# Attention on one core: values held still in two column halves of the array, row sums by 32-column groups

## The reference, cut to what matters

```python
AT_HEADS, AT_KV_HEADS, AT_HD, Q_BLOCK = 8, 2, 64, 128
keys = concat([rope(ak), cache_k])          # 1024 + 128 keys, 2 key-value heads
def one(qblk):                              # 128 queries, 4 query heads per key-value head
    s = einsum('bqkgd,bskd->bkgqs', qblk, k) * D ** -0.5
    p = softmax(s, axis=-1)
    return einsum('bkgqs,bskd->bqkgd', p, v)
```

## Time and profile before

| what | value |
|---|---|
| median of three runs | 2380.0 us (2376.93 to 2381.06) |
| span of the profiled execution, first to last instruction | 2375.2 us |
| TensorE busy | 97% of the span |
| VectorE, ScalarE, GpSimd busy | 58%, 34%, 9% |
| the attention loop | 1156 to 1401 us |

### The profile page before, as it was taken

How to read it: one execution, slowest core, us unless ns; L and a number is a source line. 1 busy time by engine, 2 the same in 40 slices (tenths; PEclk the granted TensorE clock), 3 DMA queues, 4 the chain that set the end, 5 groups by cost and what they waited for, 6 DMA issues and landing times. The chain is left out here.

```text
span 2375.2 us, 44414 instructions
## 1 busy us (share of the span) xinstructions
PE 2301.3 (97%) x17959; PEld 2126.0 (90%) x17959; DVE 1388.8 (58%) x2203; ACT 810.0 (34%) x1398; POOL 224.3 (9%) x244
## 2 busy tenths in 40 slices
PE   6999999999999899999999999998999999999997
PEld 5887779999999889998999989877999999998886
DVE  4331266533554467665455546768676676667877
ACT  5321132213333233223344444325222223234444
POOL 0000000001110011112211101000121121120001
PEclk9999999999999999999999999999999999999999
DMA  6324632236452532214100228421222232259534
GB/s 279 120 84 182 224 111 107 101 135 202 157 173 85 196 107 90 80 67 158 44 18 13 88 107 311 159 91 62 78 105 91 73 109 91 73 177 273 131 100 124
DMA packets 126864, 295.40 MB, mean 124 GB/s; under 512 B 19808, under 2 KB 63280, under 8 KB 117376
## 3 DMA queue, kind: packets, MB, share of 16 engines
q1 hardware_dynamic: 93360, 236.31, 29.7%
q10 hardware_dynamic: 29392, 41.82, 4.8%
q0 software_dynamic: 3968, 15.21, 1.7%
HBM read 207.83 MB, written 85.53 MB: 124 GB/s over the span
## 5 line engine op out<-in xcount | busy, mean ns | idle before, releaser
L62 PE MATMUL ps<-prj_w,h_hi 128*128 128x512 f32 (+1 forms) x864 | 255.4, 380 | 4.1 <-DVE h_lo L755 4.1
L62 PE MATMUL ps<-h_hi,fill_whi 128*128 128x384 f32 x672 | 235.6, 351 | 4.7 <-ACT fill_st L1119 2.4
L62 PE MATMUL ps<-h_lo,fill_whi 128*128 128x384 f32 x672 | 226.5, 337 | 3.8 <-issue 3.8
L62 PE MATMUL ps<-wt 128*128 128x320 f32 (+2 forms) x1046 | 227.2, 327 | 2.3 <-DVE merged L3205 1.3
L62 PE MATMUL ps<-h_hi,fill_wlo 128*128 128x384 f32 x672 | 226.6, 337 | 0.1
L62 PE MATMUL ps<-ys,mergedr 128*128 128x256 f32 (+1 forms) x1056 | 219.6, 297 | 0.4 <-issue 0.4
L62 PE MATMUL ps<-zb,mergedr 128*128 128x320 f32 (+2 forms) x764 | 200.1, 326 | 4.9 <-issue 2.7
L62 PE MATMUL ps<-zb,wt 128*128 128x384 f32 (+3 forms) x758 | 200.2, 325 | 0.0
L62 PEld LDWEIGHTS ps<-prj_w,h_hi 128*128 128x128 f32 x864 | 158.3, 191 | 42.8 <-issue 10.6
L62 PEld LDWEIGHTS ps<-wt 128*128 128x128 f32 x1046 | 179.6, 189 | 16.7 <-issue 2.6
L62 PEld LDWEIGHTS ps<-ys,mergedr 128*128 128x128 f32 x1056 | 174.5, 190 | 0.7 <-issue 0.7
(11 more groups left out here) (502 smaller groups left out, 4675.5 us busy)
## 6 DMA issues: line engine op xcount, KB each, us to landing
wraw<-in_w_ffn_in SPq DMA_DIRECT2D x22, 1024.0 KB, 5.3
prj_raw<-in_w_ada SPq DMA_DIRECT2D x16, 1024.0 KB, 6.0
fill_raw<-in_w_fill SPq DMA_DIRECT2D x30, 512.0 KB, 4.4
wtf<-a_dram SPq DMA_DIRECT2D x55, 256.0 KB, 2.7
bg_dram<-fill_st ACTq DMA_DIRECT2D x72, 192.0 KB, 2.0
xf<-bg_dram POOLq DMA_DIRECT2D x24, 576.0 KB, 7.1
tok_dram<-prj_tst ACTq DMA_DIRECT2D x45, 256.0 KB, 2.1
prj_raw<-in_w_tok SPq DMA_DIRECT2D x10, 1024.0 KB, 6.9
```

Of the source, the lines that this page charges most:

```text
L62: mm = pe.matmul(out, lhs[a], rhs[b], start=first and n == 0, stop=last and n == 2, skip_group_check=onto)
```

## The change

The loop now runs over query tiles, not over groups: a step takes one key block for both key-value heads. In `values` the 64 value columns of a key-value head are stationary and 512 columns of exponentials move; head 0 writes partitions 0 to 63 and head 1 partitions 64 to 127 of the same bank, so the result comes out already turned. The row sums, which the column of ones gave before, come from `sums`: 32 columns of ones are stationary, and the 128 columns of exponentials of query head `a` move into partitions `32a` to `32a + 31`. After a tile VectorE inverts the sums of all heads (`inverted`), `spread_sums` copies each row to the 64 partitions of its head by eight small matmuls, ScalarE copies the unscaled result out (`output`), VectorE multiplies it by the spread sums (`normed`), and SP, not ScalarE, issues the transfer. Per tile, the queries' turn, the shifts' turn and all eight `shift_scores` for the next tile stand between the steps. So before the first tile all eight `shift_scores` are done, not four, each between two halves of a `branch` unit. Scores have two PSUM banks, not three. The hardware loops are written out.

```diff
+        def rows_out(s):                                   # SP
+            sp.dma_start(g.y_dram[...], yt[s % 2][:]).then_inc(sem[f"yout{s % 2}"], 16)
...
-            def scores(n, kv, j):
-                pe.wait_ge(sem["ex"], 9 * n + j + 1)
-                out, at = ps[:, ST + j % 3, :], slice(j * P, j * P + P)
+            def scores(i, kv, j):
+                u = 2 * NT * i + 2 * j + kv
+                if u >= 2:
+                    pe.wait_ge(sem["ex"], u - 1)
+                if j == 0:
+                    pe.wait_ge(sem["pte"], turn(i, 2 + kv) + 1)
+                out, at = ps[:, ST + kv, :], slice(j * P, j * P + P)
...
-            def values(n, kv, j):
-                pe.wait_ge(sem["ex"], 9 * n + j + 4)
-                for a in range(G):
-                    mm = pe.matmul(ps[:, OB, a * H1:a * H1 + H1], pt[j % 3][:, a * P:a * P + P], va[:, j, kv, :],
-                                   start=j == 0 and a == 0, stop=j == NT - 1 and a == G - 1)
+            def values(i, j):
+                n = NT * i + j
+                pe.wait_ge(sem["ex"], 2 * n + 2)
+                for kv in range(KV):
+                    mm = pe.matmul(ps[kv * HD:kv * HD + HD, OB, :], va[:, j, kv, 0:HD], pt[n % RING][:, kv, :],
+                                   start=j == 0, stop=j == NT - 1)
+            def sums(i, j):
+                n = NT * i + j
+                if j == 0 and i:
+                    pe.wait_ge(sem["rc"], i)
+                for kv in range(KV):
+                    for a in range(G):
+                        mm = pe.matmul(ps[32 * a:32 * a + 32, SB, kv * P:kv * P + P], ones[:], pt[n % RING][:, kv, a * P:a * P + P],
+                                       start=j == 0 and kv == 0, stop=j == NT - 1 and kv == KV - 1)
+            def spread_sums(i):
+                pe.wait_ge(sem["rc"], i + 1)
+                for a in range(G):
+                    for kv in range(KV):
+                        mm = pe.matmul(ps[kv * HD:kv * HD + HD, PT, a * P:a * P + P], spread[:, a, :], rs[:, kv, :],
+                                       start=True, stop=True)
...
-            def output(u, i):
-                for t in range(4):
-                    mm = pe.transpose(ps[:, PT, t * P:t * P + P], y[:, 2 * t:2 * t + 2, :]..., g.ident[:])
+            def tile(i):
+                more = i < LAST
+                for j in range(NT):
+                    for kv in range(KV):
+                        scores(i, kv, j)
+                    if more and j < 2:
+                        queries(i + 1, j)
+                    if i and j == 2:
+                        spread_sums(i - 1)
+                    if more and j == 5:
+                        shifts(i + 1, 0)
+                    if more and 1 <= j < NT - 1:
+                        shift_scores(i + 1, j - 1)
+                    if j:
+                        values(i, j - 1)
+                        sums(i, j - 1)
+                    if more and j == NT - 2:
+                        shift_scores(i + 1, AH - 1)
+                if more:
+                    shifts(i + 1, 1)
+                values(i, NT - 1)
+                sums(i, NT - 1)
...
+            for u in (21, 22, 23):
+                shift_scores(0, 2 * u - 40)
+                if u == 23:
+                    shifts(0, 0)
+                branch(range(u, u + 1), (0, 2))
+                shift_scores(0, 2 * u - 39)
+                branch(range(u, u + 1), (2, 4))
+            shifts(0, 1)
+            for i in range(LAST + 1):
+                tile(i)
             pe.wait_ge(sem["b1lo"], 5)
-            branch_tile(pe, ps, 0, [g.wt[:, 2 * n, :] for n in range(2)], g.ys0)
+            branch_tile(pe, ps, 0, [g.wt[:, 2 * n, :] for n in range(2)], g.ys0, thirds=range(0, 2))
+            spread_sums(LAST)
+            branch_tile(pe, ps, 0, [g.wt[:, 2 * n, :] for n in range(2)], g.ys0, thirds=range(2, 3))
...
+            def exponentials(i, j):                        # ScalarE
+                n = NT * i + j
+                if n >= RING:
+                    act.wait_ge(sem["sums"], n - RING + 1)
+                for kv in range(KV):
+                    act.wait_ge(sem["s2"], 2 * n + kv + 1)
+                    act.activation(pt[n % RING][:, kv, :], ps[:, ST + kv, :], ACT.Exp, scale=QS).then_inc(sem["ex"], 1)
...
+            def inverted(i):                               # VectorE
+                v.wait_ge(sem["sums"], NT * i + NT)
+                v.reciprocal(rs[:].rearrange("p k n -> p (k n)"), ps[:, SB, 0:KV * P]).then_inc(sem["rc"], 1)
+            def normed(i):
+                v.wait_ge(sem["spread"], i + 1)
+                v.wait_ge(sem["evict"], i + 1)
+                v.tensor_tensor(x, x, ps[:, PT, :], ALU.mult).then_inc(sem["norm"], 1)
```

More of the change, by code:

```diff
@@ L1897, in attention @@
         kn = ph.sb("kn", [P, NT, KV, HD])
+        with ExitStack() as later:
+            over = lambda name, shape, dt=F32: later.enter_context(nc.sbuf_tensor(f"att_{name}", shape, dt))
+            pt = [over(f"pt{i}", [P, KV, G * P]) for i in range(RING)]
+            qt1, qm1 = ([over(f"{n}1{kv}", [P, G * P], F32R) for kv in range(KV)] for n in ("qt", "qm"))
         k2 = ph.sb("k2", [P, NT, KV, HD])
@@ L2002, in rope @@
                     gp.wait_ge(sem["rope"], 6 * n + 3 * e + 3)
-            rope(0)
-            with gp.Fori(0, 7) as i:
-                rope(i + 1)
+            for n in range(LAST + 1):
+                rope(n)
         def turn_queries(pe, kv, bank):
@@ L2085, in _, with queries @@
             mm.then_inc(sem["comm"], 1)
-            def queries(u, kv):
-                pe.wait_ge(sem["pte"], u) if not (isinstance(u, int) and u == 0) else None
-                turn_queries(pe, kv, PT).then_inc(sem["ptm"], 1)
-            def shift_scores(n, kv, a):
-                if not (isinstance(n, int) and n + a == 0):
-                    pe.wait_ge(sem["mx"], 4 * n + a)
+            def queries(i, kv):
+                if i == 0 and kv == 0:
+                    pe.wait_ge(sem["cdone"], 1)
+                else:
+                    pe.wait_ge(sem["pte"], turn(i, kv))
+                pe.wait_ge(sem["part"], 2 * i + kv + 1)
+                turn_queries(pe, kv, PT).then_inc(sem["ptm"], 1)
@@ L2095, in shift_scores @@
+            def shift_scores(i, h):
+                kv, a = h // G, h % G
+                if a == 0:
+                    pe.wait_ge(sem["pte"], turn(i, kv) + 1)
+                if i or h:
+                    pe.wait_ge(sem["mx"], AH * i + h)
                 for c in SHIFTS:
-                    mm = pe.matmul(ps[:, c, 0:TH], qt[kv][:, a * P:a * P + P], kt[0][:, kv, c * TH:c * TH + TH],
+                    mm = pe.matmul(ps[:, c, 0:TH], qt[i % 2][kv][:, a * P:a * P + P], kt[0][:, kv, c * TH:c * TH + TH],
@@ L2129, in group @@
[L2129 to L2133, removed]
-                if more:
[L2135 to L2154, removed]
@@ new lines, in _ @@
+            queries(0, 0)
+            shift_scores(0, 0)
+            queries(0, 1)
+            branch(range(20, 21), (0, 2))
+            shift_scores(0, 1)
+            pe.wait_ge(sem["pte"], 2)
+            for t in range(4):
+                mm = pe.transpose(ps[:, PT, t * P:t * P + P], y[:, 2 * t:2 * t + 2, :].rearrange("p h d -> p (h d)"), g.ident[:])
+            mm.then_inc(sem["ptm"], 1)
+            branch(range(20, 21), (2, 4))
+            for u in (21, 22, 23):
[5 more added lines that the diff above has]
+                branch(range(u, u + 1), (2, 4))
@@ L2225, in _ @@
             store(range(19, 20))
[L2226 to L2243, removed]
@@ L2245, in group, with queries @@
-            def group(i, kv, more):
-                n = 2 * i + kv
-                if more:
-                    queries(use(i, 0 if kv == 0 else 3), 1 - kv)
-                for j in range(NT):
-                    act.wait_ge(sem["s2"], 9 * n + j + 1)
-                    act.wait_ge(sem["pv"], 9 * n + j + 1)
-                    act.activation(pt[j % 3][:], ps[:, ST + j % 3, :], ACT.Exp, scale=QS).then_inc(sem["ex"], 1)
-                    if j == 3 and kv == 0:
-                        output(use(i, 1), i)
-                    if isinstance(i, int) and kv == 0 and j in (1, 4, 6, 7):
-                        ahead((1, 4, 6, 7).index(j))
-                    if isinstance(i, int) and kv == 1 and j in (1, 4):
-                        ahead(4 + j // 4)
-                if more:
-                    shifts(use(i, 2 if kv == 0 else 4), 1 - kv)
+            def queries(i, kv):
+                act.wait_ge(sem["ptm"], turn(i, kv) + 1)
+                act.activation(qt[i % 2][kv][:], ps[:, PT, :], ACT.Copy).then_inc(sem["pte"], 1)
@@ new lines, in output, with tile @@
+            def output(i):
+                act.wait_ge(sem["pv"], i + 1)
+                if i:
+                    act.wait_ge(sem[f"yout{(i + 1) % 2}"], 16 * ((i - 1) // 2 + 1))
```

(35 more changed lines are left out.)

189 lines of the change are left out of this document (100 added, 89 removed).

## The result

The changed kernel takes 2388.26 us (median of four runs, 2387.85 to 2390.7), where the kernel before took 2378.47 in runs beside it (2376.13 to 2381.06). The ratio is 1.0049 with a 95% interval of 1.0037 to 1.0060: slower by half a per cent. The forecast was 2386, between 2374 and 2397. The profiled execution has a span of 2386.2 us, 11.0 more than before, and a time of its own of 2387.97.

What follows compares the result with a forecast made beforehand. The prediction took the attention loop to be bound by TensorE's work. Steps -4, rest of a tile 6.6 and 0.7, ahead of the loop 2.6, the end -0.7 and 0.7: about 6 us over 2380, so 2386; range 2374 to 2397.

Steps and rivals of the forecast that it cites:

- Scores, 0.235 each: In a step's scores: the same four matmuls at 0.235 us each, 0.94 us.
- Values, two rounds of 0.43: In a step's values: four passes of 512 moving columns, two halves side by side, 0.86 us.
- Sums, 0.43: In a step's sums: sixteen passes of 128 columns on four groups, four rounds of 0.11, 0.43 us.
- Whole array to columns and back, 0.33: In each step: the array empties and the first load after it is not hidden, about 0.33 us for two changes.
- Halves to groups, 0.11 between bounds of 0 and 0.24: Between values and sums: changing from halves to 32-column groups costs 0.11 us a step, though no row shows it.
- The two rivals with a free change: Free only between values and sums: 2378 us, chance 0.27; no change of shape costs anything: 2352 us, chance 0.12.
- `spread_sums`, 1.19 a tile: Between full-array matmuls: eight rounds of 0.11, 0.86, and 0.33 for changes; 9.5 us more; tiles 31 to 32 us apart.
- The reciprocal, at most 1.3 us: VectorE's `inverted`, 256 columns: between 0.35 and 1.3 us, run during steps 0 and 1, costing nothing.
- Ahead of the loop: Before tile 0: TensorE waits for VectorE's maxima, about 0.5 us at a time; 2.6 us more.
- The end, 0.7 us more of the barrier: After the loop: last spread, `normed` and transfer outlast the covering `branch_tile` work; barrier waits 0.7 us longer.
- The sum: 6 forecast: Whole kernel: -4 + 6.6 + 0.7 + 2.6 - 0.7 + 0.7, about 6 us more.

## Why the prediction was right, step by step

- Scores, 0.235 each: as forecast. Values, two rounds of 0.43: right, by the 0.86 us that a further block costs and by the 0.85 us a step that one half costs more. Sums, 0.43: measured 0.44.
- Whole array to columns and back, 0.33: measured 0.10 on the way in and 0.14 + 0.10 on the way back, 0.34. The reading of the last 0.10 as part of a change was wrong: behind L463 the second full row came 0.11 late, but a late second row (0.32 for 0.235) also stands in the steps of the kernel before, where no shape changes. The sum is not hurt by it, since the old step's 1.36 us hold their 0.32 and the new step has its 0.34. The way in and back was given back as well where it was left out: 0.35 us a tile when the spread moved into the visit.
- Halves to groups, 0.11 between bounds of 0 and 0.24: measured 0.15, and taking this change away gave 9 to 10 us back. The two rivals with a free change fall with that. That the 0.11 came near was in part luck: it was taken over from what was left for another change, as no row showed this one. It is most of why a step takes 2.73 and not 2.67, near 4 us in 72 steps: the largest of the terms that were mis-sized.
- `spread_sums`, 1.19 a tile: its row lasts 1.02 with 0.10 ahead of it and 0.10 on the first `shift_scores` behind it. The tiles are 31.70 us apart, within the 31 to 32 given.
- The reciprocal, at most 1.3 us by the rows of 4 and 6 columns: it takes 1.76 us for 256 columns. The bound was wrong; hidden in the loop, it costs nothing there.
- Ahead of the loop, TensorE waits for maxima 0.4 to 0.5 us at a time, as forecast. Not seen was VectorE's split, which waits for TensorE and has a maximum queued behind it: 1.2 us, given back when it was moved.
- The end, 0.7 us more of the barrier: 1.25, of which 0.9 went when the transfer came earlier.
- The sum: 6 forecast; 4 for the steps, 1.2 for the split and 0.6 for the barrier make 11.8, and the three stages measured 11.5. All three misses went the same way, so none made up for another. In the medians the difference is 9.8.

The mechanism was right: the loads are gone, the old value rows were bound by them (33 columns cost what 65 did), and changing the array's shape costs nearly as much as they did. Why halves to groups costs 0.15 and the way in 0.10 stays open.

## What to carry to other kernels

An exchange of operands that moves work into column groups is priced with every change of the array's shape that it puts into a step, not only with its passes: here a step took 0.49 us beyond its passes, 0.39 of it at changes of shape, and that ate a gain of 0.48 (2.72 before, 2.24 for the passes alone). Give neighbouring work one shape even at twice the instructions, and when a visit is left out, first see whose wait the removed work was covering. A wait on one engine's queue is paid by what stands behind it, so look at what is queued there.

## What was not expected of the hardware

- Eight loads of 32 columns with two moving operands in four quarters take the same 0.86 us as four loads of 64 columns in two halves.
- VectorE's reciprocal took 1.76 us for 256 columns, 6.9 ns a column, where a multiplication of 512 columns took 0.69.
- GpSimd added 1024 columns in 2.47 us, while VectorE's maxima that ran beside it stayed at 1.36.
